# State-space blocks: the eight output products of a block issued in turn for the two halves of the partitions

## The chip, the core and the metric

One core of a Trainium2 chip runs the whole kernel, in one launch. The metric is the device time of the launch in microseconds, and the median of several executions counts.

## What is computed

The reference runs two decoder blocks of two layers each over 512 tokens of width 1024. Only the first layer's mixer matters here, a diagonal state-space model (64 groups of 16 channels, 64 complex states in each group):

```
u  = rmsnorm(h, norm_mix[0])
xr, xi = scan over the tokens of  x <- a * x + (bb * u)       # complex, per group and state
y  = einsum('ghn,btgn->btgh', c_re, xr) - einsum('ghn,btgn->btgh', c_im, xi) + d * u
y  = gelu(y)
ab = y @ ssm_w_glu ;  h = h + ab[..., :dm] * sigmoid(ab[..., dm:])
```

After it come two multilayer perceptrons, attention, a Mamba-2 layer and differential attention, which the change doesn't touch.

## The kernel before

The 512 tokens are taken as 64 steps of 8 tokens (`NSTEP`, `STEP`), and the 64 groups as 8 blocks of 8 groups (`NBLK`, `GB`). In one block the rows of a tile are 8 tokens x 16 channels = 128. The output of a group has two parts. The direct part takes the tokens inside a step: the inputs `Ub` of the group (128 x 64, the stationary operand) times a triangular table `Tm` (128 x 128). The other part takes what the steps before have left: the states `Wb` (128 x 64, stationary) times the table `TC` (128 x 128). Both are float32 matmuls that accumulate in the same 64 x 128 piece of the PSUM bank 4. Groups 0 to 3 of the block write partitions 0 to 63 of the bank (`ybank(1)`), groups 4 to 7 write partitions 64 to 127 (`ybank(2)`), so that the stationary operand of a product takes one half of TensorE's columns. A float32 matmul with 128 columns of moving data stands in the trace as two records; the 16 products of a block are 32 records.

`s5_tensor` is TensorE's program for this stage. Its `step(T)` issues, for T from 1 to 7: the transposes and the direct tables of block T (`transposed` L777, `direct` L787, for each half), the turning of the outputs of block T-2 (L821), a rotation of the states `Zb` of block T-1 (L826, called JZ), the step sums of block T (`step_sums` L796), the output products of block T-1 (L843 the direct part, L844 the part of the states), and the rotation of the sums of block T (`rotated` L802). At T = 8 there is no block to start. The output products of the last block lie between four pieces of the first weight tile of the gated linear unit (`pe_unit` with `U_GLU`, lines L183 to L185): two slices of it before them, two after them, then the turning of the last outputs (L821), and then the rest of the unit. From there on TensorE goes from weight tile to weight tile.

On the other engines: ScalarE copies the sums out (`s_kept` L529), makes the sine and cosine tables of a block (L508, L510, L512), copies the two halves of the outputs to `Ysb` (L559) in the order first half, second half, and takes the gelu (L548, L550). VectorE makes the tables `TB` (L644, L652, L653), the fractions of a turn (L662, L663), the scan (L728 to L735) and the states `Wb` (L742, L744). GpSimd makes the angles (L438), the inputs `Ub` (L434) and the table `TC` (L427 to L429). SyncE loads the weight tiles (L2407) and scatters `Ksb` to `Tm` (L413).

All waits are written by hand as counts on semaphores. `s5_out` counts JZ, Y1 and Y2 of each block; `Y1` and `Y2` tell ScalarE that the first and the second half of the outputs stand in the bank. `s5_y_kept` tells TensorE that ScalarE has copied them. `Y2` also frees `TC` (three buffers), `Ub` (two) and `Wb` for the blocks that follow.

Of the kernel before, what the change touches and what calls it, by code (L numbers as in the profile page):

```python
# [12 lines left out]
LANES, TOK, DM = 128, 512, 1024  # L13
# [79 lines left out]
def program(nc, a):  # L93
    ctx = ExitStack()
    with ctx:
        base = [(nc.sbuf_base + 255) // 256 * 256]

        def put(name, shape, dt=F32, at=None):
            size = int(np.prod(shape[1:])) * 4
            if at is None:  # L100
                at = base[0]
                base[0] += (size + 31) // 32 * 32
                assert base[0] <= nc.sbuf_usable_end, (name, base[0], nc.sbuf_usable_end)
            return nc.alloc_sbuf_tensor_at(name, shape, dt, offset=at)

        def sem(name):
            return ctx.enter_context(nc.semaphore(name))
# [4 lines left out]
        h = put("h", [LANES, KT, TOK])  # L112
# [21 lines left out]
        def C(name, lo=0, hi=None, rows=LANES):  # L134
            a0, a1 = CC[name]
            return const[0:rows, a0 + lo:(a1 if hi is None else a0 + hi)]
# [37 lines left out]
        def pe_unit(e, u0, j, n4, xh, xl, first=None, ks=range(KT)):  # L174

            b = bk[(u0 + j) % 4]
            w = (u0 + j) % RING
            e.wait_ge(w_split, after(u0, j, n4, 1))
            e.wait_ge(bank_free, after(u0, j, n4, 1))
            for k in ks:  # L180
                if first is not None:
                    e.wait_ge(*first(k))
                e.matmul(b, w_hi[:, w, k], xh[:, k], start=(k == 0), stop=False)  # L183
                e.matmul(b, w_hi[:, w, k], xl[:, k], start=False, stop=False)  # L184
                last = e.matmul(b, w_lo[:, w, k], xh[:, k], start=False, stop=(k == KT - 1))  # L185
            if ks[-1] == KT - 1:
                last.then_inc(unit_done, 1)
# [99 lines left out]
        def own_buf(name, shape, dt=F32, lanes=LANES):  # L287
            at[0] = (at[0] + 31) // 32 * 32
            t = put(name, [lanes] + list(shape), dt, at=at[0])
            at[0] += int(np.prod(shape)) * 4  # L290
            assert at[0] <= nc.sbuf_usable_end, name
            return t
# [13 lines left out]
        Ub = own_buf("Ub", [2, GB, NSTEP])  # L306
        Wb = own_buf("Wb", [GB, NSTEP])
# [3 lines left out]
        Tm = own_buf("Tm", [2, GB, STEP, SH])  # L311
# [12 lines left out]
        TC = own_buf("TC", [3, GB, STEP + 1, SH])  # L324
# [25 lines left out]
        s5_y_kept = Steps(sem("s5_y_kept"), "Y1 Y2", ahead=4)  # L350
# [4 lines left out]
        s5_out = Steps(sem("s5_outputs"), "JZ Y1 Y2", ahead=4)  # L355
# [31 lines left out]
        def ready(s, n):  # L387

            return lambda k: (s, n + (k + 1))
# [194 lines left out]
        def ybank(k):  # L584
            return bank[4][64 * (k - 1):64 * k, :]
# [175 lines left out]
        def s5_tensor(e):  # L761
            for counters in (s5_sums, s5_tt, s5_k, s5_js, s5_out, s5_turned):
                counters.open(e)
            e.wait_ge(const_loaded, 16)
            for m in range(KT):
                e.wait_ge(squared, m + 1)
                e.matmul(bk[4], C("ones"), squares[m % 4], start=(m == 0), stop=(m == KT - 1)).then_inc(acc_ready, 1)
            e.wait_ge(acc_ready, KT)
            e.sem_inc(norm_mm, 1)
            e.wait_ge(zeroed, 2)  # L770

            def transposed(q, ks=(1, 2)):
                for k in ks:
                    e.wait_ge(s5_tables.sem, s5_tables.at("TBa" if k == 1 else "TBb", q))
                    e.wait_ge(s5_st_kept.sem, s5_st_kept.at(f"ST{3 - k}", q - 2 + k))
                    for g in range(4):
                        last = e.transpose(bank[0][:, g * LANES:(g + 1) * LANES], TB[:, 4 * k - 4 + g].rearrange("p s h -> p (s h)"), C("ident"))  # L777
                    s5_tt.took(f"ST{k}", last)

            def direct(q, ks=(1, 2)):  # L780
                e.wait_ge(s5_pooled.sem, s5_pooled.at("TC", q))
                e.wait_ge(s5_direct.sem, s5_direct.at("Kd", q - 1))
                for k in ks:
                    e.wait_ge(s5_k_kept.sem, s5_k_kept.at(f"K{k}", q - 1))
                    for g in range(4):
                        gg = 4 * k - 4 + g
                        last = e.matmul(bank[5][64 * (k - 1):64 * (k - 1) + SH, g * LANES:(g + 1) * LANES], TB[:, gg, 0], TC[:, q % 3, gg, 0:STEP].rearrange("p s h -> p (s h)"), start=True, stop=True)  # L787
                    s5_k.took(f"K{k}", last)

            def step_sums(q):  # L790
                e.wait_ge(s5_inputs.sem, s5_inputs.at("U", q))
                e.wait_ge(s5_st_kept.sem, s5_st_kept.at("ST2", q))
                e.wait_ge(s5_kept.sem, s5_kept.at("Sx", q - 1))
                e.wait_ge(s5_states.sem, s5_states.at("pr1", q - 1))
                for g in range(GB):
                    last = e.matmul(bank[2][:, g * NSTEP:(g + 1) * NSTEP], ST[:, g], Ub[:, q % 2, g], start=True, stop=True)  # L796
                s5_sums.took("S", last)

            def rotated(q):
                e.wait_ge(s5_kept.sem, s5_kept.at("Sx", q))  # L800
                e.wait_ge(s5_states.sem, s5_states.at("W", q - 1))
                s5_js.took("JS", e.matmul(bk[3], C("turn"), Sx[:, q % 2].rearrange("p g c -> p (g c)"), start=True, stop=True))  # L802

            def step(T):
                if T == 0:
                    transposed(T)
                    direct(T)
                    step_sums(T)
                    rotated(T)
                elif T < NBLK:  # L810
                    for k in (1, 2):
                        transposed(T, (k,))
                        direct(T, (k,))
                q = T - 2
                if 0 <= q < NBLK:
                    e.wait_ge(s5_y_kept.sem, s5_y_kept.at("Y2", q))
                    e.wait_ge(s5_gelu.sem, s5_gelu.at("g", q - 1))
                    for t in range(STEP):

                        turned = e.transpose if t else e.matmul  # L820
                        last = turned(bank[7][:, t * NSTEP:(t + 1) * NSTEP], Ysb[:, t].rearrange("p g h -> p (g h)"), C("ident", hi=NSTEP, rows=NSTEP))  # L821
                    s5_turned.took("YT", last)
                q = T - 1
                if 0 <= q < NBLK:
                    e.wait_ge(s5_states.sem, s5_states.at("Z", q))
                    s5_out.took("JZ", e.matmul(bk[3], C("turn"), Zb[:, :, :].rearrange("p g c -> p (g c)"), start=True, stop=True))  # L826
                if 0 < T < NBLK:
                    step_sums(T)
                q = T - 1
                if 0 <= q < NBLK:  # L830
                    t, z = q, q % 2
                    if T == NBLK - 1:
                        rotated(T)
                    if T == NBLK:
                        pe_unit(e, U_GLU, 0, 0, x1h, x1l, ready(x_ready, 0), range(0, 2))
                    e.wait_ge(s5_states.sem, s5_states.at("W", t))
                    e.wait_ge(t_loaded[z], 16 * STEP * (2 + q // 2))
                    for k in (1, 2):
                        e.wait_ge(s5_y_kept.sem, s5_y_kept.at(f"Y{k}", q - 1))
                        for g in range(4):  # L840
                            gg = 4 * k - 4 + g
                            o = ybank(k)[:, g * LANES:(g + 1) * LANES]
                            e.matmul(o, Ub[:, z, gg], Tm[:, z, gg].rearrange("p s h -> p (s h)"), start=True, stop=False)  # L843
                            last = e.matmul(o, Wb[:, gg], TC[:, q % 3, gg, 1:].rearrange("p s h -> p (s h)"), start=False, stop=True)  # L844
                        s5_out.took(f"Y{k}", last)
                    if T == NBLK:
                        pe_unit(e, U_GLU, 0, 0, x1h, x1l, ready(x_ready, 0), range(2, 4))
                if 0 < T < NBLK - 1:
                    rotated(T)
            for T in range(NBLK + 2):  # L850
                step(T)
# [1785 lines left out]
```

## Time and profile before

| | |
|---|---|
| median of 3 runs | 2039.29 us (2038.96 to 2041.32) |
| the profiled execution | 2046.67 us, of which 2044.9 us are the span of the instructions |
| TensorE busy | 95% of the span |
| VectorE, ScalarE, GpSimd busy | 61%, 44%, 21% |
| mean granted clock of TensorE | 0.98 of full speed |
| state-space blocks, first to last output product | 47.8 to 135.0 us |

Engines: PE is TensorE's matmuls, PEld its weight loads, DVE VectorE, ACT ScalarE, POOL GpSimd. A matmul's duration in a row holds its way through the array, so that rows of one kind overlap: the pace is the distance between two starts. PEclk is the share of TensorE's full clock that was granted in a stretch.

### The profile page before, as it was taken

How to read it: one execution, taken by the hardware profiler on the slowest of the kernel's cores; microseconds unless marked ns; L12 is line 12 of the kernel's file. 1: busy time of each engine (PE TensorE's matmuls, PEld its weight loads, DVE VectorE, ACT ScalarE, POOL GpSimd, SP SyncE). 2: the span in 40 equal slices, each digit the busy share in tenths (PEclk: the TensorE clock that was granted, in tenths of full speed). 3: DMA queues.
4: the chain of work that ended last, by engine and by line, in shares of the span. 5: the costliest groups of instructions: out<-in, count | busy, mean ns of one | idle time of the engine just before them, and what ended most of it. 6: DMA issues, size and time to landing. Idle time of an engine off the chain costs nothing.

```text
span 2044.9 us, 27151 instructions
## 1 busy us (share of the span) xinstructions
PE 1942.3 (95%) x9462; PEld 1557.6 (76%) x9462; DVE 1254.5 (61%) x1792; ACT 895.4 (44%) x1504; POOL 421.6 (21%) x281
## 2 busy tenths in 40 slices
PE   5999999999999999999999999999999998999996
PEld 3778788888887666788888887788878786777774
DVE  8954444343468887534343488877667755777654
ACT  4864433232345454423232344455355542466650
POOL 6852100000142002100000251632122225000003
PEclk8999999999999989999999999999999998999998
DMA  5213333333332112232332332222222222222221
GB/s 197 46 36 126 93 93 100 94 94 101 93 95 90 42 42 61 84 100 95 94 101 93 99 97 72 63 73 67 78 62 73 70 67 65 88 63 63 71 64 62
DMA packets 54524, 166.99 MB, mean 82 GB/s; under 512 B 13217, under 2 KB 13345, under 8 KB 53921
## 3 DMA queue, kind: packets, MB, share of 16 engines
q1 hardware_dynamic: 54432, 165.78, 26.8%
q8 instruction: 57, 0.93, 0.2%
q14 instruction: 35, 0.28, 0.0%
HBM read 161.30 MB, written 2.10 MB: 80 GB/s over the span
## 4 chain that ended last, share of the span: by engine, by line
PE 75%; DVE 9%; ACT 6%; issue 3%; DMA 2%; POOL 2%; DVEq 0%; POOLq 0%; SPq 0%; PEldq 0%
PE bank L183 14%; PE bank L185 14%; PE bank L184 14%; PE bank L1531 4%; PE bank L1532 4%; PE bank L1533 4%; DMA raw<-in_w_dram 2%; PE bank L2137 2%; PE bank L2139 2%; PE bank L2138 2%; PE bank L1546 1%; PE bank L1547 1%; PE bank L1548 1%; ACT w_hi L195 1%; PE bank L1574 1%
## 5 line engine op out<-in xcount | busy, mean ns | idle before, releaser
L203 DVE TENSOR_TENSOR w_lo<-raw,w_hi 128x1024 fp32r<-128x1024 f32 x286 | 368.0, 1287 | 442.9 <-ACT w_hi L195 441.3
L195 ACT ACTIVATE w_hi<-raw 128x1024 fp32r<-128x1024 f32 x289 | 305.6, 1058 | 603.3 <-DMA raw<-in_w_dram 603.3
L183 PE MATMUL bank<-x1h,w_hi 128*128 128x512 f32 x680 | 267.5, 393 | 6.5 <-DVE x1l L218 6.5
L184 PE MATMUL bank<-x1l,w_hi 128*128 128x512 f32 x680 | 265.3, 390 | 0.0
L185 PE MATMUL bank<-x1h,w_lo 128*128 128x512 f32 x680 | 265.1, 390 | 0.0
L183 PE MATMUL bank<-x0h,w_hi 128*128 128x512 f32 x640 | 250.4, 391 | 0.0
L185 PE MATMUL bank<-x0h,w_lo 128*128 128x512 f32 x640 | 249.0, 389 | 0.0
L184 PE MATMUL bank<-x0l,w_hi 128*128 128x512 f32 x640 | 249.0, 389 | 0.0
L232 POOL TENSOR_TENSOR sq<-h 128x512 f32 (+1 forms) x64 | 81.0, 1266 | 771.6 <-DVEq L948 659.3
L1531 PE MATMUL bank<-x1h,w_hi 128*128 128x512 f32 x384 | 156.6, 408 | 0.0
L183 PEld LDWEIGHTS bank<-x1h,w_hi 128*128 128x128 f32 x680 | 128.0, 188 | 35.2 <-DVE x1l L218 7.8
L1532 PE MATMUL bank<-x1l,w_hi 128*128 128x512 f32 x384 | 151.9, 396 | 0.0
L1533 PE MATMUL bank<-x1h,w_lo 128*128 128x512 f32 x384 | 151.8, 395 | 0.0
L184 PEld LDWEIGHTS bank<-x1l,w_hi 128*128 128x128 f32 x680 | 128.1, 188 | 27.5 <-issue 1.0
L185 PEld LDWEIGHTS bank<-x1h,w_lo 128*128 128x128 f32 x680 | 128.1, 188 | 26.6
L183 PEld LDWEIGHTS bank<-x0h,w_hi 128*128 128x128 f32 x640 | 120.1, 188 | 25.9 <-issue 1.2
L184 PEld LDWEIGHTS bank<-x0l,w_hi 128*128 128x128 f32 x640 | 120.1, 188 | 25.8 <-issue 0.7
L185 PEld LDWEIGHTS bank<-x0h,w_lo 128*128 128x128 f32 x640 | 120.1, 188 | 24.9
L234 POOL TENSOR_TENSOR acc<-acc,sq 128x512 f32<-128x512 f32 x64 | 102.8, 1606 | 5.0
L927 DVE TENSOR_TENSOR x1l<-a,x1h 128x512 f32 x64 | 44.3, 693 | 92.7 <-ACT a L917 92.7
L915 ACT ACTIVATE x1h<-t 128x512 f32 x64 | 40.5, 632 | 130.9 <-DVE t L925 130.9
L1531 PEld LDWEIGHTS bank<-x1h,w_hi 128*128 128x128 f32 x384 | 73.6, 192 | 18.1 <-issue 1.9
(391 smaller groups left out, 3636.0 us busy)
## 6 DMA issues: line engine op xcount, KB each, us to landing
raw<-in_w_dram SPq DMA_DIRECT2D x289, 512.0 KB, 3.5
h<-in_xT_dram SPq DMA_DIRECT2D x1, 2048.0 KB, 12.1
Ur<-in_xu_dram SPq DMA_DIRECT2D x8, 256.0 KB, 2.7
out_dram<-h SPq DMA_DIRECT2D x8, 256.0 KB, 2.2
const<-in_const_dram SPq DMA_DIRECT2D x1, 1028.0 KB, 14.6
B_st<-in_B_dram SPq DMA_DIRECT2D x1, 1024.0 KB, 6.1
C_st<-in_C_dram SPq DMA_DIRECT2D x1, 1024.0 KB, 14.1
p_in<-in_pT_dram SPq DMA_DIRECT2D x1, 1024.0 KB, 5.5
```

What stands on the lines that cost most here:

```text
L183: e.matmul(b, w_hi[:, w, k], xh[:, k], start=(k == 0), stop=False)
L184: e.matmul(b, w_hi[:, w, k], xl[:, k], start=False, stop=False)
L185: last = e.matmul(b, w_lo[:, w, k], xh[:, k], start=False, stop=(k == KT - 1))
L195: e.activation(w_hi[:, z], raw[:, z], ACT.Copy).then_inc(hi_split, 1)
L203: e.tensor_tensor(w_lo[:, z], raw[:, z], w_hi[:, z].bitcast(F32), ALU.subtract).then_inc(w_split, 1)
L232: e.tensor_tensor(one(sq[:, :]), tile(h, m), tile(h, m), ALU.mult).then_inc(squared, 1)
L234: e.tensor_tensor(acc[:, :], acc[:, :], sq[:, :], ALU.add).then_inc(acc_ready, 1)
L927: e.tensor_tensor(tile(x1l, m), one(a32[:, :]), tile(x1h, m).bitcast(F32), ALU.subtract).then_inc(a_ready, 1)
L1531: e.matmul(b, w_hi[:, w, k], x1h[:, k], start=(k == 0), stop=False)
L1532: e.matmul(b, w_hi[:, w, k], x1l[:, k], start=False, stop=False)
L1533: last = e.matmul(b, w_lo[:, w, k], x1h[:, k], start=False, stop=(k == KT - 1))
L2137: e.matmul(b, w_hi[:, w, k], xh[:, k], start=(k == 0), stop=False)
```

## The change

Before, the half k is the outer loop: for one half the four groups, and for each group the direct product and behind it the product of the states; then the other half. Now the group g is the outer loop, and inside it the direct products of group g of both halves are issued first, then the products of the states of both halves. The same 16 products with the same operands write to the same places, and each piece of the bank gets its direct product first. Two waits differ: TensorE now waits for the copy of both halves of the outputs of the block before (`Y2` of `s5_y_kept`) ahead of all 16 products, and the count `Y1` rises with the second last product instead of in the middle.

```diff
-                    for k in (1, 2):
-                        e.wait_ge(s5_y_kept.sem, s5_y_kept.at(f"Y{k}", q - 1))
-                        for g in range(4):
+                    e.wait_ge(s5_y_kept.sem, s5_y_kept.at("Y2", q - 1))
+                    for g in range(4):
+                        o = [ybank(k)[:, g * LANES:(g + 1) * LANES] for k in (1, 2)]
+                        for k in (1, 2):
                             gg = 4 * k - 4 + g
-                            o = ybank(k)[:, g * LANES:(g + 1) * LANES]
-                            e.matmul(o, Ub[:, z, gg], Tm[:, z, gg].rearrange("p s h -> p (s h)"), start=True, stop=False)
-                            last = e.matmul(o, Wb[:, gg], TC[:, q % 3, gg, 1:].rearrange("p s h -> p (s h)"), start=False, stop=True)
-                        s5_out.took(f"Y{k}", last)
+                            e.matmul(o[k - 1], Ub[:, z, gg], Tm[:, z, gg].rearrange("p s h -> p (s h)"), start=True, stop=False)
+                        for k in (1, 2):
+                            gg = 4 * k - 4 + g
+                            last = e.matmul(o[k - 1], Wb[:, gg], TC[:, q % 3, gg, 1:].rearrange("p s h -> p (s h)"), start=False, stop=True)
+                            if g == 3:
+                                s5_out.took(f"Y{k}", last)
```

## Rows read from the trace of the kernel before

**Rows 1.** The chain of waits, 56 to 70 us: start, us, what.
```profile
56.70 1.13 PE bank L826 x2
57.83 1.74 PE bank L796 x16
...
68.86 1.13 PE bank L826 x2
```
**Rows 2.** Timeline of TensorE, 59 to 62 us: start, us, instruction, count.
```profile
59.49 0.43 PE L843 MATMUL bank<-Tm,Ub 128*64 128x128 f32 x2
...
60.42 0.38 PE L843 MATMUL bank<-Tm,Ub 128*64 128x128 f32 x2
...
60.85 0.44 PE L843 MATMUL bank<-Tm,Ub 128*64 128x128 f32 x4
61.07 0.44 PE L844 MATMUL bank<-TC,Wb 128*64 128x128 f32 x4
61.35 0.38 PE L843 MATMUL bank<-Tm,Ub 128*64 128x128 f32 x2
```
**Rows 3.** The timeline of all engines, 63 to 75 us; in brackets the idle time before.
```profile
63.18 1.20 ACT L559 ACTIVATE Ysb<-bank 64x512 f32<-64x512 f32 x2
64.41 0.60 ACT L518 ACTIVATE ST<-bank 128x512 f32<-128x512 f32 x1
65.22 0.66 PE L777 MATMUL bank<-const,TB 128*128 128x128 f32 x4
...
68.86 1.13 PE L826 MATMUL bank<-Zb,const 128*128 128x512 f32 x2 [1.21 <-DVE Zb L735]
...
71.62 2.64 POOL L429 TENSOR_TENSOR TC<-TC,TCt 128x1152 f32<-128x1152 f32 x1
```
**Rows 4.** The same timeline around the last block's products, 125 to 137 us.
```profile
125.44 0.59 ACT L559 ACTIVATE Ysb<-bank 64x512 f32<-64x512 f32 x1 [0.71 <-PE bank L844]
...
127.91 1.76 PE L826 MATMUL bank<-Zb,const 128*128 128x512 f32 x2 [0.97 <-DVE Zb L735]
...
131.96 0.43 PE L843 MATMUL bank<-Tm,Ub 128*64 128x128 f32 x2
...
135.22 0.50 PE L183 MATMUL bank<-x1h,w_hi 128*128 128x512 f32 x1
...
135.33 0.60 ACT L559 ACTIVATE Ysb<-bank 64x512 f32<-64x512 f32 x1 [0.72 <-PE bank L844]
...
136.81 0.87 PE L821 MATMUL bank<-const,Ysb 64*128 64x64 f32 x9
```
**Rows 5.** Timeline of TensorE in the Mamba layer, where halves change with each head.
```profile
1308.38 0.45 PE L1586 MATMUL bank<-decays,xdt 128*64 128x128 f32 x4 [0.19 <-DVE decays L1768]
1308.65 0.39 PE L1588 MATMUL bank<-cs,state 128*64 128x128 f32 x4
1308.87 0.44 PE L1586 MATMUL bank<-decays,xdt 128*64 128x128 f32 x4
1309.09 0.44 PE L1588 MATMUL bank<-cs,state 128*64 128x128 f32 x4
1309.46 0.50 PE L1531 MATMUL bank<-x1h,w_hi 128*128 128x512 f32 x1
```
**Rows 6.** Busy us by stretch: length, PE, PEld, DVE, ACT, POOL, PEclk, DMA, GB/s.
```profile
116.00:120.00 4.00, 2.88 (x23) 2.27 (x22) 3.71 (x13) 3.00 (x4) 0.89 (x1) 1.00 0.08 12
...
124.00:128.00 4.00, 2.35 (x24) 1.97 (x21) 3.63 (x12) 3.16 (x5) 3.78 (x2) 1.00 0.03 4
128.00:132.00 4.00, 4.00 (x9) 2.24 (x9) 2.21 (x5) 0.87 (x2) 1.55 (x1) 0.57 0.00 0
```
**Rows 7.** The chain of waits again, two pieces at the lower clock.
```profile
34.74 3.69 PE bank L796 x16
...
129.67 0.43 PE bank L183
```
**Rows 8.** Busy time of a longer stretch behind the blocks, columns as in rows 6.
```profile
145.00:200.00 55.00, 55.00 (x244) 45.55 (x243) 23.84 (x26) 23.21 (x26) 13.81 (x10) 1.00 0.37 123
```

## Prediction

> **What bounds the kernel now.** I read three views in this order. The page says that TensorE is busy for 95% of the span, so I first ask whether it is also what sets the pace in the stage that the change touches. The chain of waits answers that [rows 1]. In the state-space blocks one turn of the chain goes JZ and the step sums on TensorE (L826, L796), the sine table on ScalarE (L508, L510), the angles on GpSimd (L438), then fractions, products and scan on VectorE (L662 to L735), and again JZ. JZ starts at 56.70 us and again at 68.86, so a turn takes 12.16 us. The reader is to see what is missing: no output product (L843, L844) stands in it. They begin at 59.49, right behind the step sums [rows 2], while ScalarE makes the tables of the next turn, and TensorE then idles for 1.21 us ahead of JZ, waiting for the scan [rows 3].
>
> At the end this is otherwise. The products of the last block start at 131.96, and the next matmul on TensorE, of the gated unit, starts at 135.22 [rows 4]. From there on TensorE has no idle time: it is busy for 55.00 of 55.00 us [rows 8]. So a microsecond taken from the last block's products is a microsecond off the time, and one taken from the seven blocks before is not.
>
> **What the new order does to one block's products.** Products of one half run one behind the other: from 60.42 to 60.85 a direct product and one of the states, four records, 0.109 us for each record and 0.218 for a product [rows 2]. In the middle, where the halves change, it is different: four records of L843 start at 60.85, four of L844 at 61.07, and the next product starts at 61.35. That is eight records in 0.50 us, where eight at 0.109 would take 0.87. The two halves run at the same time there. The Mamba layer has the order that the change introduces: its heads change halves each time. Sixteen records, from 1308.38, are followed by the next matmul at 1309.46, so 1.08 us with start and handover, and from one pair of products (four records) to the next pass 0.22 us: 0.109 for each step of two records, one in each half [rows 5].
>
> The block now: 131.96 to 135.22 is 3.26 us [rows 4]. After: the Mamba burst's 1.08 us for sixteen records, and sixteen more in eight steps of 0.109, 0.87, give 1.95 us. I take this price, since it is measured on alternating halves. Saving in a block: 3.26 - 1.95 = 1.31 us. The bounds: 1.5 us if the steps alone counted (3.26 - 16 x 0.109), and a loss of 0.4 if the halves did not overlap at all and the overlap in the middle, 0.37 us, were lost too.
>
> The Trainium skill has a rule that speaks against this. Its page "TensorE: Matmul & The Clock Gate", Part 3, says that weight loads overlap matmuls in flight only when the row groups differ, and that matmuls start in strict program order. Halves of the columns share all rows. By that rule weights of the second half would wait for the first, and the saving of 1.31 would be nothing; that is rival (b) below. The trace disagrees: four L843 records stand ahead of L844's in the middle of the block, though the program has the last L844 of the first half ahead of the second half's L843.
>
> **Blocks 0 to 6.** TensorE gets through the products 1.31 us sooner. What follows on TensorE starts sooner only in part: the second transposes (65.22) need the copy of the first (L518), which ScalarE begins at 64.41, right behind the two copies of the outputs, and ends at 65.01 [rows 3]. So they start about 0.15 us sooner and the rest of the gain is idle time there. The direct tables also need `TC` from GpSimd, which ends at 71.62 + 2.64 = 74.26 [rows 3]; the products of that turn would end at 59.49 + 12.16 + 1.95 = 73.6, and L802 and the first transposes come before the tables. JZ stays where the scan puts it. Idle time ahead of JZ grows from 1.2 to about 1.4 us. Worth on the chain: 0. If that cover were gone, each block would give up to 1.31 us.
>
> **The waits.** TensorE now waits for the copy of both halves at the head. For the last block that copy ended at 125.44 + 0.59 = 126.03, and the products start at 131.96 [rows 4]; in the other blocks 7 us lie between (the copies end at 64.38, the products start at 71.65) [rows 2, 3]. Cost 0, nothing queues behind it. `Y1` used to come in the middle, 1.3 us ahead of `Y2`, and now comes at the end. The copy of the last products to be issued begins 0.11 us behind the next matmul's start (135.33, 135.22); in the new order that matmul starts at 131.96 + 1.95 = 133.91, so the first copy begins near 134.0, the two stand in one piece of 1.20 us [rows 3] and end near 135.2, and the turning L821 needs both. TensorE has six matmuls of the gated unit in between, which took 136.81 - 135.22 = 1.59 us [rows 4]; they end at 133.91 + 1.59 = 135.50. The cover is 0.3 us, so the cost is 0; bounds 0 and 0.3. `Y2` comes sooner for GpSimd and VectorE, who don't stand at it.
>
> Here too a page bears on it. The Trainium skill, "TensorEngine Tiling (Array Packing)", PSUM Bottleneck, says that tiling speeds up TensorE but not the emptying of PSUM, which may become the bound. The rows give it 1.20 us of copying against 1.59 us of cover, so that by the trace it comes close and stays hidden.
>
> **The clock.** Where TensorE has more idle time the granted clock can fall. It is 1.00 (2.4 GHz) in each of the 21 stretches of 4 us from 44 to 128 us, of which two stand in the rows, and its mean is 0.57 from 128 to 132, behind a stretch in which TensorE was busy for 2.35 of 4 us. A stretch with 2.88 of 4 did not bring it down [rows 6]. The new order lowers the busy time of a turn by 1.3 us of 12.15, and ahead of the last JZ the products of the block before end 1.3 us sooner, which widens the gap in which it fell. At the lower clock a matmul of the unit takes 0.43 us [rows 7] and not 1.59/6 = 0.27 [rows 4]: six of them, and JZ's 1.76 for 1.13 [rows 1, 4], cost 1.0 + 0.6 = 1.6 us, part of it under VectorE's work. The profiled execution has paid this already. So the unknown is between 0 and about 1.6 us more for executions that do not pay it now, and as much again if the lower clock lasts into the last products (1.95 us, doubled). I take 0 for the likeliest and keep 3 us for the range.
>
> **Sum.** Against the profiled execution, 2046.67 us (span 2044.9): last block -1.31, blocks 0 to 6 0, waits 0, clock 0: 2045.4. The profiled execution stands 7.4 us above the median of the runs shown, which this change has no reason to alter. Against the median: 2039.29 - 1.31 = 2038.0.
>
> **Rivals.**
> (a) The gain of the last block is eaten, by the clock (0 to 1.6 us more) or by the copies: 2038.6 to 2041. For it: the clock did fall there, with the gap now wider. Against: where it fell before, it costs nothing new. Chance 0.20.
> (b) The halves do not overlap, so the change does not do what it says: 2039.29 + 0.4 = 2039.7. Against it speak eight records in 0.50 us [rows 2] and the Mamba rows [rows 5]. Chance 0.04.
> (c) Slower: the clock falls inside the blocks, ahead of JZ, where TensorE now idles longer. The step sums stand in the chain and took 3.69 us at the lower clock [rows 7] against 1.74 [rows 1], and JZ 1.76 against 1.13 [rows 1, 4]: up to 2.6 us for each block in which it falls. It turns the sign at the first fall, and exceeds 0.2% (4.1 us) from the third: 3 x 2.6 - 1.3 = 6.5, at most 6 x 2.6 - 1.3 = 14, so 2045.8 to 2053. Against: the clock held through stretches with little work. One or two falls leave it inside 0.2%. Chance of three or more 0.07.
> (d) Faster by more: TensorE's queue sets the turns of the blocks after all, and each of eight blocks gives 1.31: 2039.29 - 10.5 = 2028.8. Against: the idle time ahead of JZ, and a chain without L843. Chance 0.04.
> The forecast itself has 0.65.
>
> **How the numbers follow.** The forecast and (a), (b) lie within 0.2% of before (4.1 us, about what a measurement of this kernel can tell from no change). With (d) faster by over 0.2% gets 0.05, with (c) slower 0.08, the rest 0.87. Range: the forecast with its term's bounds and the spread of the runs before (2.4 us) goes from 2035.2 to 2040; (a), (b) and one fall of (c) reach 2042.6. Left out are (d) and most of (c), about 0.13.
>
> **What would show it.** In the profile after: from the first L843 to the next other matmul 1.9 to 2.0 us in each block, the L843 and L844 rows in fours; 12.1 to 12.2 us from JZ to JZ; idle time ahead of JZ at 1.3 us or more; L183 behind the last products about 1.3 us sooner, and the same 1.3 us at the first unit of 145 us. PEclk tells (a) and (c): a fall ahead of 124 us is (c), with L796 above 1.8 us. I would be wrong if the turn got shorter than 12.0, or if two copies in a piece made L821 wait.

## The result, and the profile after

The changed kernel took 2049.95 us (median of 10 runs, 2046.38 to 2055.69), the kernel before 2040.37 us (10 runs, 2035.92 to 2043.81). The ratio is 1.0046, with a 95% interval of 1.0033 to 1.0059: slower by 9.6 us from median to median, where 1.3 us less was forecast. The profiled execution took 2052.09 us, with a span of 2050.3.

In the profile after, the products L844 of before stand in line L846. The last block first, as rows of TensorE's timeline (start, us, instruction):

```profile
140.25 0.46 PE L843 MATMUL bank<-Tm,Ub 128*64 128x128 f32 x4
140.54 0.39 PE L846 MATMUL bank<-TC,Wb 128*64 128x128 f32 x4
...
142.17 0.50 PE L183 MATMUL bank<-x1h,w_hi 128*128 128x512 f32 x1
...
143.76 0.87 PE L821 MATMUL bank<-const,Ysb 64*128 64x64 f32 x9
```

The records come in fours, and from the first product to the gated unit's matmul pass 142.17 - 140.25 = 1.92 us, against 3.26 before [rows 4] and 1.95 in the forecast. The turning L821 comes 1.59 us later, as before, so that the two copies in one piece stay hidden. But the block begins at 140.25 and not at 131.96. The time was lost ahead of it. The chain of waits shows where (start, us, what):

```profile
57.06 2.76 DVE bank L737
...
70.77 2.55 DVE bank L737
...
84.28 1.47 DVE bank L737
...
96.72 2.60 DVE bank L737
...
110.27 1.78 DVE bank L737
...
123.03 1.89 PE bank L826 x2
124.92 3.32 PE bank L796 x16
128.27 0.61 ACT Sx L529
128.92 2.08 PE bank L802 x2
131.00 0.62 PE bank L843 x4
```

Two things stand in it that the chain before did not have. From 57.06 to 123 us it holds VectorE's instructions and nothing of TensorE, with L737, the first product behind the scan, at 2.76, 2.55, 1.47, 2.60 and 1.78 us, where it took 0.70 before (0.72 in the turn at 56.7). And from 123.03 on it holds TensorE: JZ (L826) takes 1.89 us and not 1.13, the step sums L796 3.32 and not 1.74 [rows 1], and the output products themselves are on it. The busy time in stretches of about a turn (length, PE, PEld, DVE, ACT, POOL, PEclk, DMA, GB/s) tells the two apart. Before:

```profile
56.70:68.90 12.20, 10.98 (x86) 8.69 (x86) 11.19 (x24) 10.25 (x16) 9.02 (x6) 1.00 0.21 46
68.90:81.00 12.10, 10.95 (x85) 8.62 (x85) 11.06 (x24) 9.75 (x17) 11.09 (x6) 1.00 0.21 45
```

After:

```profile
57.00:71.00 14.00, 12.81 (x86) 10.28 (x87) 13.43 (x25) 8.61 (x14) 8.56 (x6) 0.76 0.19 41
71.00:84.50 13.50, 11.31 (x86) 8.76 (x86) 12.97 (x24) 10.29 (x17) 12.09 (x7) 0.87 0.19 43
84.50:97.00 12.50, 9.76 (x86) 7.37 (x86) 11.97 (x24) 11.54 (x16) 9.98 (x7) 1.00 0.20 45
97.00:110.50 13.50, 9.64 (x86) 7.23 (x86) 12.97 (x24) 11.72 (x17) 11.79 (x7) 1.00 0.20 43
110.50:123.00 12.50, 9.49 (x85) 7.09 (x84) 11.98 (x23) 9.74 (x15) 7.78 (x5) 1.00 0.13 24
123.00:136.50 13.50, 11.43 (x62) 8.40 (x63) 6.63 (x17) 6.68 (x10) 8.50 (x4) 0.62 0.13 24
```

The granted clock (the 1.00 is 2.4 GHz, and in the stretches below it part of the time was at 1.2) is below 1 in three of these six stretches, where it was 1.00 in every turn of the kernel before. In the first one where it holds, TensorE is busy for 9.76 of 12.5 us, against 10.98 of 12.2.

Measured from JZ to JZ (starts at 57.08, 70.80, 84.30, 96.74, 110.30, 123.03 and 136.28) the turns take 13.72, 13.50, 12.44, 13.56, 12.73 and 13.25 us. Before, five took 12.15 or 12.16 us and the last 10.44. So in this execution 5.2 us went in the five turns whose chain is VectorE's with the long L737, and 2.8 us in the last, whose chain is TensorE at the lower clock. Three of the five lie in stretches with a granted clock of 1.00, and the turn of 13.56 us is one of them: there the long L737 did it without the clock. In the first two both were there, and the chain shows only the longer.

The clock first fell at 58 us, in the turn in which TensorE had stood idle for 2.15 us ahead of JZ:

```profile
57.08 1.12 PE L826 MATMUL bank<-Zb,const 128*128 128x512 f32 x2 [2.15 <-DVE Zb L735]
58.04 3.17 PE L796 MATMUL bank<-Ub,ST 128*128 128x64 f32 x16
```

I call the two suspects the clock (theory B in the expectations) and the collision (theory A). The collision looks like this in the timeline of VectorE and GpSimd:

```profile
56.64 2.62 POOL L429 TENSOR_TENSOR TC<-TC,TCt 128x1152 f32<-128x1152 f32 x1
...
57.06 2.76 DVE L737 TENSOR_TENSOR bank<-Zb,cosb 128x512 f32<-128x512 f32 x1
```

L737 begins 0.42 us behind L429 and ends 0.56 us after it (59.82, 59.26). Before, it was the other way round: L737 began at 56.69, L429 at 56.92, and it was L429 that took longer, 2.96 us. The Trainium skill, "SBUF — State Buffer", section "Who interferes with whom", describes a port pair that VectorE and GpSimd share, held for the whole instruction by whichever starts first, when a VectorE instruction has two inputs in SBUF and GpSimd's reads SBUF. L737 is such a one (`Zb`, `cosb`), and the trace agrees: 2.76 us behind L429, 0.72 ahead of it. Before, GpSimd had waited 0.49 us for block 0's products ahead of its inputs at 51.23; now they started at 50.95, although the first JZ of the blocks came 0.37 us later (45.34, 44.97). Counted from that JZ, L737 begins at 11.72 us in both kernels, and L429 at 11.95 before and 11.30 now, 0.65 us sooner.

### The profile page after: what moved, and what is told of

Same layout as the page of the kernel before. It is cut to its first block, busy times and chain, and to the rows that moved or that the text cites. A ratio compares the mean times of both kernels' runs of the same rounds, so it can differ in the third digit from the quotient of the medians.

```text
span 2050.3 us, 27151 instructions
## 1 busy us (share of the span) xinstructions
PE 1937.5 (94%) x9462; PEld 1551.4 (76%) x9462; DVE 1263.2 (62%) x1792; ACT 895.4 (44%) x1504; POOL 421.6 (21%) x281
## 4 chain that ended last, share of the span: by engine, by line
PE 73%; DVE 13%; ACT 6%; DMA 3%; issue 3%; POOL 2%; DVEq 0%; POOLq 0%; SPq 0%; PEldq 0%
PE bank L183 14%; PE bank L185 14%; PE bank L184 14%; PE bank L1534 4%; PE bank L1536 3%; PE bank L1535 3%; DMA raw<-in_w_dram 3%; PE bank L2140 2%; PE bank L2142 2%; PE bank L2141 2%; PE bank L1549 1%; ACT w_hi L195 1%; PE bank L1550 1%; PE bank L1551 1%; DVE w_lo L203 1%
## 5 line engine op out<-in xcount | busy, mean ns | idle before, releaser
L195 ACT ACTIVATE w_hi<-raw 128x1024 fp32r<-128x1024 f32 x289 | 305.7, 1058 | 602.6 <-DMA raw<-in_w_dram 602.5
```

The lines of the kernel that those rows point to most:

```text
L195: e.activation(w_hi[:, z], raw[:, z], ACT.Copy).then_inc(hi_split, 1)
```

## The experiments

All ratios are to the kernel before, in runs on the same chip: 12 executions of each kernel (6 of e9_filler, 7 of e18_change_again) against 29 to 35 of the kernel before. "Low clock" is the time at the lower clock in the mean of a kernel's executions: twice (1 - mean granted clock) times the span. For the kernel before it was 63 to 69 us in the four comparisons, most of it outside the state-space blocks; for the changed kernel in its first measurement it was 94.6 us. What the change adds lies in the blocks: from 44 to 145 us the mean granted clock is 0.98 in the profile before, and 0.88 and 0.86 in the two profiles of the changed kernel. "Turn" is the time from JZ to JZ; before, it is 12.15 or 12.16 us, and 10.44 us for the last.

| kernel | ratio (95% interval) | low clock, us | before beside it |
|---|---|---|---|
| e18_change_again | 1.0035 (1.0016 to 1.0054) | 89 | 65 |
| e1_last | 0.9994 (0.9977 to 1.0011) | 62 | 65 |
| e2_not_first | 1.0027 (1.0012 to 1.0042) | 84 | 65 |
| e3_pool_waits | 1.0036 (1.0018 to 1.0053) | 92 | 65 |
| e4_twice | 1.0016 (0.9999 to 1.0033) | 71 | 65 |
| e5_wait_twice | 1.0013 (0.9999 to 1.0027) | 66 | 63 |
| e6_before_pool_waits | 1.0008 (0.9996 to 1.0020) | 67 | 63 |
| e9_filler | 1.0054 (1.0037 to 1.0071) | 77 | 63 |
| e10_filler_wait | 1.0024 (1.0009 to 1.0038) | 67 | 63 |
| e12_fewer | 1.0032 (1.0016 to 1.0047) | 91 | 69 |
| e13_direct_twice | 1.0008 (0.9991 to 1.0024) | 74 | 69 |
| e8_before_twice | 0.9991 (0.9978 to 1.0004) | 57 | 69 |
| e15_front | 0.9992 (0.9978 to 1.0005) | 57 | 69 |
| e7_first | 1.0015 (1.0002 to 1.0028) | 70 | 65 |
| e17_last_twice | 0.9997 (0.9984 to 1.0010) | 63 | 65 |
| e16_last_twice_end | 0.9994 (0.9982 to 1.0007) | 61 | 65 |

**The change in parts.** The new order only where a condition on the block `q` holds, else the old one:

```diff
+                    if q == NBLK - 1:      # e1_last;  q > 0 in e2_not_first;  q == 0 in e7_first
```

> The new order in the last block alone, the old one in blocks 0 to 6. Theory A (the new order lets GpSimd's tables start ahead of VectorE's product L737, which then waits for GpSimd; this happens in blocks 0 to 6 and comes from the signal Y2 that arrives sooner): the loss is gone and the saving of the last block stays, ratio to before 0.999 to 1.000, L737 at 0.70 us in nearly all blocks. Theory B (the clock falls because TensorE has more idle time in each block): also no loss, since blocks 0 to 6 are as before; so 0.999 to 1.000 too. If the ratio is above 1.003, the loss comes from the last block, and both are wrong.

Measured 0.9994, no loss, and in its profile the last block's products take 133.68 - 131.78 = 1.90 us:

```profile
131.78 0.44 PE L844 MATMUL bank<-Tm,Ub 128*64 128x128 f32 x4
...
133.68 0.50 PE L183 MATMUL bank<-x1h,w_hi 128*128 128x512 f32 x1
```

So the loss comes from blocks 0 to 6. The 1.3 us of the last block are inside the interval of 0.9994, not shown by it.

> The old order in block 0 alone, the new one in blocks 1 to 7. GpSimd waited for an output product only once before (0.49 us, for block 0's Y2). Theory A: with block 0 as before, GpSimd's second inputs wait again, the first collision at 57 us does not come, and VectorE and GpSimd keep the order of before from turn to turn: ratio 0.998 to 1.001, L737 at 0.70 us. Theory B: seven of eight blocks still leave TensorE idle longer: ratio 1.003 to 1.006, as with the whole change.

Measured 1.0027 and 84 us of low clock, while its profile has L737 at 0.70 us in six of eight blocks and never above 0.96. Its turns of the new order take 12.15 us at a granted clock of 1.00 (TensorE busy for 9.62 us of them), and 12.77 and 14.67 us at 0.91 and 0.73. So a loss is there without the collision: B. And the same idle time does not bring the clock down in every turn.

> The new order in block 0 alone. Its Y2 comes sooner, so GpSimd does not wait (0.49 us before) and starts its tables sooner: if that is what puts GpSimd ahead of VectorE, L737 shows waits of 1 to 2.8 us in the blocks from 57 us on, as with the change, while TensorE's busy time from block 1 on is as before and the clock holds. Price of the collision by itself: about 0.001 if the waits cost what the comparison with and without GpSimd's wait showed (1.0046 against 1.0036), 0.003 if all of the 8 us less the slack showed.

Measured 1.0015. The collision did come, and once: the duration of L737 in nanoseconds (min/median/max, first and last start) is

```profile
L737 DVE TENSOR_TENSOR bank<-Zb,cosb x8: 700/701/2746, 44.2 to 131.0; 128x512 f32<-128x512 f32 x8
```

so that the earlier signal of block 0 does bring it about, but it did not go on from turn to turn, as I had expected. The clock fell in that profile too, at 58.7 us, in the same turn, which took 14.30 us, so this kernel does not give the collision's price by itself.

**The two suspects, taken away singly and together.** GpSimd waits ahead of L428 until L737 is done:

```diff
+                if q >= 2:
+                    e.wait_ge(s5_states.sem, s5_states.at("po1", q - 2))
                 s5_pooled.next(e, q).took("TC2", tt(TCt[:, :, :, :], ...
```

> The whole change, and GpSimd waits ahead of the second product of its table (L428) until VectorE's L737 of the running turn is done. Theory A: L737 takes 0.70 us in every block, the turn is 12.2 us again, ratio 0.998 to 1.001. Theory B: the clock falls as with the change, ratio 1.003 to 1.006.

Measured 1.0036 with 92 us of low clock: the loss stays. Its profile has no collision left and the falls of the clock all the same. L737 stands in line L739 there; the second fence is its turns:

```profile
L739 DVE TENSOR_TENSOR bank<-Zb,cosb x8: 700/700/781, 44.3 to 135.1; 128x512 f32<-128x512 f32 x8
```

```profile
57.50:71.40 13.90, 12.83 (x85) 10.38 (x85) 11.13 (x24) 8.70 (x14) 10.65 (x6) 0.75 0.18 40
71.40:83.70 12.30, 10.14 (x86) 7.82 (x86) 11.27 (x24) 10.08 (x18) 10.78 (x7) 0.94 0.21 47
83.70:98.40 14.70, 13.86 (x87) 10.80 (x86) 11.02 (x24) 10.99 (x16) 10.69 (x6) 0.70 0.17 39
```

The turn takes 12.3 us where the clock is near 1 and 13.9 to 14.7 where it is 0.70 to 0.75. Of the other three, two take 12.15 us at 1.00 and the last 13.24 us at 0.61. So the clock lengthens a turn without the collision, as the collision does without the clock in the changed kernel's first profile. The second suspect is taken away by more work for TensorE:

```diff
             def rotated(q):
                 ...
+                e.matmul(bk[3], C("turn"), Sx[:, q % 2].rearrange("p g c -> p (g c)"), start=True, stop=True)
                 s5_js.took("JS", e.matmul(bk[3], C("turn"), Sx[:, q % 2].rearrange("p g c -> p (g c)"), start=True, stop=True))
```

> The whole change, and the rotation L802 is issued twice (the second writes the same values), so that TensorE's busy time of a turn is about what it was before, while Y2 still comes sooner. Theory A: GpSimd still starts sooner, L737 still waits: ratio 1.003 to 1.006. Theory B: the granted clock holds at 1.00 in blocks 1 to 6 as before, ratio 0.999 to 1.001.

Measured 1.0016, between what the two expected, with 71 us of low clock instead of 90 to 95: 0.86 us more work in each turn seems to have given back some 4 to 6 us (1.0035 or 1.0046 to 1.0016), with intervals that overlap. The collision stays: its profile has three turns of 13.26, 12.68 and 13.28 us at a granted clock of 1.00, with L737 at 2.31, 1.72 and 2.33 us on the chain, and only then a turn of 14.29 us at 0.76.

> The whole change, with L802 issued twice and GpSimd's wait. Each alone gave 1.0016 and 1.0036, the change 1.0046. If clock and collision both cost, and separately: 0.9990 to 1.0005. If the collision costs nothing: 1.0016 as with L802 twice alone.

> The kernel before with L802 issued twice: the price of the filler itself. It adds 0.96 us to TensorE's queue in each turn, where 1.2 us were idle ahead of JZ: 1.000 to 1.001 by every theory; with 0.001 the experiment with the filler on the changed kernel had restored nearly all.

> The kernel before, with GpSimd's wait for L737 ahead of L428. Control for the wait: its own cost, if it costs nothing 0.999 to 1.001. If it costs, so much of the time of the changed kernel with this wait is the wait's and not the clock's.

Measured 1.0013, 0.9991 and 1.0008. With L802 twice the collision's removal brings 1.0016 to 1.0013, without it 1.0046 (or 1.0035, in its second measurement) to 1.0036. None of these steps is outside its uncertainty, and the wait itself may cost up to 1.0020. In the profile with both taken away, every turn is back at 12.15 or 12.16 us (the last at 10.44) with a granted clock of 1.00 and VectorE's product at 0.70 us. The second L802 costs nothing that can be seen, and on the kernel before it lowers the low clock from 69 to 57 us. Its turns, in the profile of the kernel before with L802 twice:

```profile
58.30:70.40 12.10, 11.80 (x88) 9.03 (x87) 11.09 (x23) 10.14 (x15) 8.92 (x6) 1.00 0.21 44
70.40:82.60 12.20, 11.81 (x88) 9.05 (x88) 11.14 (x24) 10.80 (x18) 11.18 (x7) 1.00 0.21 48
```

**Is it the pairing, or the missing busy time?** Two kernels change the one without the other. In blocks 0 to 6 of the old order six of eight direct products are left out:

```diff
+                            direct_too = g == 0 or q == NBLK - 1
+                            if direct_too:
                                 e.matmul(o, Ub[:, z, gg], Tm[:, z, gg]..., start=True, stop=False)
-                            last = e.matmul(o, Wb[:, gg], TC[...], start=False, stop=True)
+                            last = e.matmul(o, Wb[:, gg], TC[...], start=not direct_too, stop=True)
```

> The old order, and in blocks 0 to 6 six of the eight direct products are left out (that part of the outputs is missing, the times of all else stay comparable), which shortens the burst by about 6 x 0.218 = 1.3 us as the new order does. Theory B (less busy time lets the clock fall, however it came about): ratio 1.002 to 1.005 with more falls of the clock in the blocks, though work was taken away. Theory C (it is the running of two halves at once that costs, by power or by the bank): 0.999 to 1.001.

and in blocks 0 to 6 of the new order each direct product is issued twice:

```diff
+                            if q < NBLK - 1:
+                                e.matmul(o[k - 1], Ub[:, z, gg], Tm[:, z, gg]..., start=True, stop=True)
                             e.matmul(o[k - 1], Ub[:, z, gg], Tm[:, z, gg]..., start=True, stop=False)
```

> The whole change, and in blocks 0 to 6 each direct product is issued twice (the second starts the sum anew, same result). Halves still run at once; the burst is 12 steps of pairs, 2.8 us and not 1.95. Theory B: most of the busy time is back, the clock falls less: ratio 0.999 to 1.002. Theory C: as with the change or worse, 1.004 or more.

Measured 1.0032 and 1.0008. The kernel with less work and no pairing in the blocks is about as slow as the change, with 91 us of low clock; the kernel with the pairing and more work is not slower than before beyond its interval. Theory C is out. But fewer products also end sooner, and `Y2` with them: the profile of that kernel has L737 at 2.75, 2.39, 1.64, 2.41 and 1.98 us in a row, so that it has both suspects, as the change has. Its turns, with nearly the clock of after the change:

```profile
57.00:71.00 14.00, 12.72 (x74) 10.16 (x75) 13.43 (x25) 8.46 (x14) 8.73 (x6) 0.76 0.19 41
71.00:84.00 13.00, 11.10 (x73) 8.39 (x72) 12.50 (x23) 10.51 (x18) 11.42 (x7) 0.87 0.19 44
...
123.00:136.00 13.00, 11.60 (x50) 8.68 (x51) 6.34 (x17) 6.63 (x10) 8.49 (x4) 0.61 0.13 23
```

**Unread matmuls as a filler.** They write rows 32 to 63 of bank 5, in which nothing is kept:

```diff
+            def keep_busy(n):
+                for _ in range(n):
+                    e.matmul(bank[5][32:64, 0:LANES], C("ident", hi=32), C("ident"), start=True, stop=True)
```

> The whole change, and in TensorE's idle time ahead of JZ six matmuls (128 x 32 times 128 x 128, about 1.3 us) that write a part of bank 5 that nobody reads; six more ahead of the turning in the last step. No signal moves. Theory B (clock): the granted clock holds through blocks 1 to 7, the steps of L796 stay at 1.75 us, ratio 0.999 to 1.001; what GpSimd's collision costs by itself remains visible in L737. Theory A (GpSimd ahead of VectorE at L737): nothing changes, 1.003 to 1.006.

> The same fillers, and GpSimd's wait for L737 ahead of L428. If both the clock (B) and the collision (A) cost, this one is the fastest of all: turn 12.2 us, no fall of the clock, the last block's 1.3 us saved, and the fall ahead of the last block's products avoided too: ratio 0.997 to 0.9995. If B alone, it equals the kernel with the fillers alone. If A alone, it equals the kernel with the wait alone, 1.0036.

Measured 1.0054 and 1.0024: a miss, though the low clock fell to 77 and 67 us. In the profile of the first the clock holds at 58.2 us, but the collision doesn't go away: that turn takes 13.71 us at 1.00, with L737 at 2.75. The idle time that I meant to fill isn't there in every turn. Where ScalarE splits the first weight tiles (L195), its copy for the second transposes comes late, and the fillers (L801 here) then stand in JZ's way, which was L826 and is L833:

```profile
81.31 0.63 PE L777 MATMUL bank<-const,TB 128*128 128x128 f32 x4 [1.74 <-ACT ST L518]
...
83.64 1.50 PE L801 MATMUL bank<-const 128*32 128x128 f32 x12
85.07 1.13 PE L833 MATMUL bank<-Zb,const 128*128 128x512 f32 x2
```

> The kernel before, and in TensorE's idle time ahead of the first direct tables (26.8 to 31.5 us) twenty matmuls (4.4 us) into a part of bank 5 that nobody reads. Theory B, turned round: the clock that falls at 29 us and stays low to 43 now holds; the step sums at 34.7 take 1.75 us and not 3.69, L802 1.1 and not 2.1, and the first JZ comes 3 to 4 us sooner: ratio 0.998 to 0.9985. If the clock on the chain were worth nothing: 1.000.

Measured 0.9992, low clock 57 us for 69. The clock held until 41.5 us and not until 29, but the first JZ came at 45.3 us, no sooner than before (45.0). The chain there had gone over to GpSimd's first tables:

```profile
36.31 2.15 POOL TCt L428
...
38.54 2.63 POOL TC L429
...
41.22 1.62 PE bank L787 x8
```

GpSimd's path was nearly as long as the one at the low clock, so that 12 us less of low clock are not seen in the time.

**The change once more, and two kernels that were meant to beat both.**

> The changed kernel itself, on the chip of this comparison: 1.003 to 1.006, and 25 to 35 us more time at the lower clock than the kernel before.

> The new order in the last block alone, and L802 issued twice in each block. Before with L802 twice gave 0.9991 and the new order in the last block 0.9994 (1.3 us, worked out). If both hold and add: 0.998 to 0.9988. If the gain of L802 twice was chance: 0.9995.

> As the one before, and four unread matmuls each ahead of the turning and ahead of JZ in the last step, where the clock fell at 128 us. Theory B: the fall there goes too, worth up to 1.6 us: 0.9975 to 0.9985. If TensorE has no idle time left there, they stand in the path, 0.9 us each: 0.999.

The change gave 1.0035, with 25 us more of low clock. This profile of it has only one collision (2.84 us), which is not on the chain, and falls of the clock in each of the stretches shown:

```profile
57.00:71.50 14.50, 14.26 (x86) 10.90 (x86) 13.09 (x24) 7.82 (x13) 7.96 (x5) 0.66 0.17 39
71.50:85.00 13.50, 11.35 (x86) 8.33 (x87) 12.08 (x26) 10.80 (x18) 12.41 (x7) 0.87 0.19 42
85.00:98.00 13.00, 10.79 (x86) 7.96 (x84) 11.12 (x23) 10.93 (x16) 10.90 (x7) 0.87 0.19 44
```

and in its chain the two levels of the step sums:

```profile
58.85 3.32 PE bank L796 x16
...
72.57 1.75 PE bank L796 x16
```

The turns, JZ to JZ, are 14.68, 13.16, 13.31, 13.11 and 13.94 us, the last 10.44. At 58.85 the step sums at the lower clock are on the chain; from 78 to 111 us it goes over ScalarE's copies, with the split of the first weight tiles (L195) in their way, and the transposes behind them.

The other two gave 0.9997 and 0.9994. In the profile of the second the clock holds at 1.00 through the last block, but the fillers stand in the path and its last turn takes 11.50 us. With half widths of 0.0013 they cannot be told from the kernel before. No kernel here beats it for certain.

## Why the prediction was wrong

**What bounds the blocks** was right for the kernel before: the chain without the output products, and TensorE idle ahead of JZ. The experiment with the new order in the last block alone (0.9994, interval 0.9977 to 1.0011) doesn't speak against it, and can't tell 1.3 us from nothing.

**The products' price** was right: 1.95 us forecast, 1.92 measured, 1.90 with the last block alone. Rival (b), no overlap, is out. The Trainium skill's rule that speaks for (b) ("TensorE: Matmul & The Clock Gate", Part 3) is not borne out here: the products of both halves took 1.92 and 1.90 us.

**The waits**, put at 0, were right in the last block. In blocks 0 to 6 this is one of the two steps that failed: the sentence that `Y2` comes sooner for GpSimd, who does not stand at it, was wrong: GpSimd stood at it once, for 0.49 us, and without this wait its L429 came ahead of VectorE's L737. I had looked only for who is held up by a signal, not for what an engine that is let go sooner runs into. The margin before was 56.92 - 56.69 = 0.23 us, and against VectorE's L737 GpSimd's L429 came 0.65 us sooner. What the sum had at 0 for the waits cost 0.3 to 1.4 us in a turn where it stood alone (12.44 to 13.56 us at a granted clock of 1.00).

**The clock** is the other step that failed, and the one that shows in the ratios. I took 0 as the likeliest and gave rival (c) 0.07; (c) happened, with its place (step sums and JZ on the chain) in the second profile and in the one with GpSimd's wait, and nearly its price. It was put at up to 2.6 us a block; without the collision a turn at 0.70 to 0.75 took 1.7 to 2.5 us more than 12.16 (13.89, 14.67), and the last one 2.8 more (13.24 for 10.44). (c) is not the whole of it: in the first profile the clock fell as well, but the chain of five turns was VectorE's. I argued that the clock had held through stretches with little work. But the rows showed only that it held with the idle time of before, and the change adds 1.3 us of idle time to each turn. In the first one all of it stood ahead of JZ (2.15 us for 0.80), where I had put 0.2. No row showed the clock with that much idle time inside a block and holding; the nearest one, ahead of 128 us, showed it falling. So the unknown should have been bounded by a fall in every block, and been the likeliest case or near it. That was a choice on my side, and not a gap in the profile.

**Blocks 0 to 6 at zero** was therefore wrong with its sign: getting through TensorE's work sooner there has a price, by the clock and by the earlier signal. The kernel with fewer products shows the same price without the pairing, though with both of these. "I would be wrong if the turn got shorter" named the wrong side; the sign of (c), a fall ahead of 124 us with L796 above 1.8 us, was named and came (58 us, 3.17 us). That the result lies in the range given for (c), 2045.8 to 2053, owes something to chance, since (c) had no collision in it. One smaller slip: by its own terms the lower end of the range is 2039.3 - 1.5 - 2.4 = 2035.4, not 2035.2.

**What stays open.** The changed kernel minus the collision is 1.0036, against 1.0046 and 1.0035 for the change in two measurements, so what the collision adds to the whole time is not measured, though single turns show it at up to 1.6 us (13.71 us at a granted clock of 1.00 in the kernel with fillers). A reason for the small difference may be that the two delays run side by side in a turn, so that taking one away leaves the other: the turn from 57 us takes 13.72 us with both and 13.89 with the clock alone. That is argued from two profiles, not shown. With a second L802, with and without GpSimd's wait, the change still stood at 1.0013 and 1.0016, with intervals that just reach 1; whether that rest is the added work, the falls that remain, or chance is not settled either. What decides whether the clock falls in a given turn is open too. And each profile is one execution: the two profiles of the changed kernel differ in where the clock falls and in how many collisions they have, and the kernel before with GpSimd's wait had a last turn of 13.92 us at 0.63 in an execution that was 6.6 us faster than the one profiled before the change.

## What to carry to other kernels

Work that sits under a wait on TensorE is not free to remove: where the engine idles in each turn of a chain, its idle time belongs in the sum with the clock's two prices for whatever TensorE does on the chain, and a fall should be among the likely cases until a row shows the clock holding with that much idle time. A speed-up of this sort is better kept to where TensorE is the bound, here the last block, whose 1.3 us were worked out and seen in the profile but not in the ratio. And when a signal comes sooner, follow the engine that it releases to the next instruction that shares something with the chain.

## What the runs showed of the hardware

Products for the two column halves of the array run at the same time when they alternate in the queue: 1.90 to 1.92 us for 32 records with the handover, against 3.26 with one half behind the other. Taking six of sixteen small products out of each of seven blocks made the kernel slower by a ratio of 1.0032 (1.0016 to 1.0047), with 22 us more at the lower clock and with the long L737 in five turns. A repeated 128 x 512 float32 matmul in each block cost nothing that could be measured (0.9991), and lowered that time by 11 us. VectorE's product of two SBUF operands, 0.70 us by itself, took up to 2.97 us when a sum of GpSimd's (L429) had started just before it, and where it had started 0.23 us ahead GpSimd's took 2.96 us and not 2.62. A turn with L737 at 2.60 us took 13.56 us at a granted clock of 1.00, against 12.16.
